# A hybrid GLA/SSD/mLSTM trunk on one core: product of decays and scores in two parts, and five small steps of the state-space loop moved between ScalarE, VectorE, SyncE and TensorE

## What is computed

```python
y, ss_f, ss_b = bidir_scan(ch, bh * dt[0], bh * dt[1], xh, log_a[0], log_a[1], init[2], init[3])
y = y + xh * d_skip[None, :, None, None]
y = y.transpose(0, 2, 1, 3).reshape(b, l, SSD_INNER) * jax.nn.silu(z)
y = rmsnorm(y.reshape(b, l, SSD_GROUPS, SSD_INNER // SSD_GROUPS), ...)
```

## Time and profile before

| | |
|---|---|
| median of three runs | 2345.26 us |
| profiled execution | 2342.83 us, of which the recorded span is 2341.1 us |
| TensorE busy in the span | 2271.2 us (97%) |
| VectorE, ScalarE, GpSimd busy | 1369.8, 905.7, 1054.2 us |
| mean granted clock of TensorE, of full speed | 0.988 |
| the loop over the heads 2 to 15 on ScalarE | 596.9 to 703.5 us from the span's start |
| start of the second half of the output projection on TensorE | 718.8 us |

### The profile page before, as it was taken

One profiled execution on the slowest core, in us unless ns is written; L12 is line 12 of the kernel. 1 busy time (PEld: TensorE's weight loads), 2 busy tenths in 40 slices (PEclk: granted clock), 3 DMA queues, 4 the chain that ended last, 5 costly groups with the idle time before them and its releaser, 6 DMA issues.

```text
span 2341.1 us, 32702 instructions
## 1 busy us (share of the span) xinstructions
PE 2271.2 (97%) x11907; PEld 1961.2 (84%) x11907; DVE 1369.8 (59%) x1750; ACT 905.7 (39%) x1979; POOL 1054.2 (45%) x815
## 2 busy tenths in 40 slices
PE   7999999999888999999999999999999999999998
PEld 6999999998437999999999999976555567888887
DVE  5995878854765457766757466653568753211113
ACT  5215435444892356746746252132330212101002
POOL 3353334324542345534534524455133135776664
PEclk9999999999899999999999999999999999999999
DMA  8953334254631134434534323354232222333332
GB/s 278 314 161 115 112 119 141 79 178 143 202 104 36 55 105 133 140 113 121 145 109 134 71 83 128 117 186 132 67 112 90 68 62 82 99 94 95 99 97 83
DMA packets 392724, 281.07 MB, mean 120 GB/s; under 512 B 33442, under 2 KB 357820, under 8 KB 392604
## 3 DMA queue, kind: packets, MB, share of 16 engines
q1 hardware_dynamic: 333420, 200.46, 28.8%
q10 hardware_dynamic: 59184, 78.99, 10.0%
HBM read 237.34 MB, written 42.07 MB: 119 GB/s over the span
## 4 chain that ended last, share of the span: by engine, by line
PE 80%; DVE 11%; ACT 5%; DMA 2%; issue 1%; POOL 1%; SPq 0%; ACTq 0%; DVEq 0%; POOLq 0%
PE PS L963 54%; PE PS L1046 4%; PE PS L1486 3%; PE PS L1684 3%; PE PS L1498 2%; PE PS L1632 2%; PE PS L1141 1%; DVE Gn L2591 1%; DVE stage L2547 1%; PE PS L1107 1%; ACT Dm L2086 1%; DVE xcr L2547 1%; ACT Db L2079 1%; PE PS L1125 1%; PE PS L1597 1%
## 5 line engine op out<-in xcount | busy, mean ns | idle before, releaser
L963 PE MATMUL PS<-act_hi,w_hi 128*128 128x384 f32 (+1 forms) x1824 | 637.6, 350 | 6.3 <-ACT act_hi L2147 2.8
L963 PE MATMUL PS<-act_hi,w_lo 128*128 128x384 f32 (+1 forms) x1824 | 630.1, 345 | 0.0
L963 PE MATMUL PS<-act_lo,w_hi 128*128 128x384 f32 (+1 forms) x1824 | 625.9, 345 | 0.0
L745 POOL TENSOR_TENSOR w_hi<-w_raw,ones 128x128 fp32r<-128x128 f32 x232 | 127.8, 551 | 1044.9 <-DMA w_raw<-in_ffn_w 406.2
L748 POOL TENSOR_TENSOR w_lo<-w_raw,w_hi 128x1024 fp32r<-128x1024 f32 (+1 forms) x232 | 559.2, 2410 | 19.4
L963 PEld LDWEIGHTS PS<-act_hi,w_hi 128*128 128x128 f32 x1824 | 343.1, 188 | 28.7 <-issue 11.6
L963 PEld LDWEIGHTS PS<-act_lo,w_hi 128*128 128x128 f32 x1824 | 342.6, 188 | 15.1 <-issue 1.2
L963 PEld LDWEIGHTS PS<-act_hi,w_lo 128*128 128x128 f32 x1824 | 343.0, 188 | 13.8
L2162 ACT ACTIVATE fprod<-mf_ring,cs 128x128 f32<-128x128 f32 x896 | 267.9, 389 | 26.6 <-DVE mf_acc L2462 26.6
L2462 DVE TENSOR_REDUCE mf_acc<-fprod 128x128 f32<-128x1024 f32 x112 | 224.9, 2020 | 86.0 <-ACT fprod L2162 86.0
L746 POOL TENSOR_SCALAR w_hi<-w_raw 128x896 fp32r<-128x896 f32 (+1 forms) x232 | 233.0, 1004 | 0.0
(11 more groups left out here) (376 smaller groups left out, 3694.1 us busy)
## 6 DMA issues: line engine op xcount, KB each, us to landing
w_raw<-in_ffn_w SPq DMA_DIRECT2D x120, 512.0 KB, 4.0
mf_ring<-in_w_mod SPq DMA_DIRECT2D x56, 512.0 KB, 3.7
w_raw<-in_a_w_in SPq DMA_DIRECT2D x44, 512.0 KB, 4.3
proj<-stage ACTq DMA_DIRECT2D x44, 384.0 KB, 4.3
w_raw<-in_b_w_up SPq DMA_DIRECT2D x32, 512.0 KB, 4.6
m_ring<-in_w_mod SPq DMA_DIRECT2D x12, 1024.0 KB, 9.1
rows<-g_d SPq DMA_DIRECT2D x16, 768.0 KB
m_raw<-in_w_mod SPq DMA_DIRECT2D x4, 2048.0 KB, 11.9
```

What stands on the lines that cost most here:

```text
L745: pool.tensor_tensor(w_hi[:, s, 0], w_raw[:, s, 0], ones[:], ALU.mult)
L963: last = pe.matmul(to[:, c0:c1], w[:, s, k, :], x[:, k, c0:c1], start=k == 0 and w is w_hi and x is hi, stop=k == kt - 1 and w is w_lo)
```

## The change

It has six parts. The product of `Dm` with `cb` becomes two instructions, of columns 0 to 1023 (counted in `m_first`) and 1024 to 2559 (`m_done`), and `pair_products` waits for them, and for `cross_done`, one after another ahead of the products that need them. `x_copies` of the pairs 2 to 7 goes to VectorE, behind `output` of the pair before. The squares of pairs 0 to 3 go to VectorE, ahead of the heads 10 to 13. The loads of `xt` for the pairs 3 to 7 go to SyncE, behind the rows of heads 6, 8, 10, 12 and 14. On ScalarE, `act_hi` of tile 0 is written before the square of pair 7. Two waits that the moved steps no longer need where they were go with them.

```diff
--- before.py
+++ after.py
@@ -411,6 +411,7 @@
         xt_in = [sem(f"ssd_xt_in{i}") for i in range(3)]
         g_out, G_OUT0 = x_in, 32
         z_late, Z_LATE0 = r_nbd, 2
+        m_first, M_FIRST0 = r_low, 2
         z_back, Z_BACK0 = tab_in, 16 * len(table_loads(a))
         b1_in, B1_IN0 = mod_in[0], 32
         rows_in, ROWS_IN0 = mod_in[1:3], 16
@@ -672,6 +673,9 @@
                         sp.wait_ge(mask_done, 2 * h - 2)
                         sp.wait_ge(back_mask, h - 1)
                         load_rows(h)
+                        if h >= 6 and h % 2 == 0:
+                            sp.wait_ge(y_mm, h // 2 - 2)
+                            sp.dma_start(xt[h // 2 % 3][:], proj0[X0 + h // 2]).then_inc(xt_in[h // 2 % 3], 16)
                         if h == 3:
                             sp.wait_ge(mm_done, n0)
                             for p in range(2):
@@ -1297,9 +1301,12 @@
                     pe.wait_ge(y_done, p - 1)
                 for c0, c1 in ((0, LAT), (LAT, T)):
                     pe.matmul(y[:, c0:c1], skip[:, p % 2], xt[p % 3][:, c0:c1], start=True, stop=False)
-                pe.wait_ge(m_done, 2 * p + 2)
-                pe.wait_ge(cross_done, 2 * p + 2)
+                pe.wait_ge(m_first, M_FIRST0 + 2 * p + 2)
                 for c in range(6):
+                    if c == 2:
+                        pe.wait_ge(m_done, 2 * p + 2)
+                    if c == 4:
+                        pe.wait_ge(cross_done, 2 * p + 2)
                     for f in range(2):
                         h = 2 * p + f
                         D = Dm[h % 4][:, c * LAT:c * LAT + LAT] if c < 4 else Dx[h % 4][:, (c - 4) * LAT:(c - 3) * LAT]
@@ -2050,8 +2057,6 @@
                 act.activation(out, bank((6, 7, 0, 1, 4, 5, 6)[i] if g else (4, 5, 4, 5, 4, 5, 7)[i]), ACT.Copy).then_inc(cb_put, 1)
 
             def x_copies(p):
-                if p >= 2:
-                    act.wait_ge(y_mm, p - 1)
                 act.activation(skip[:, p % 2], ident[:], ACT.Copy, scale=dcol[:, p:p + 1]).then_inc(skip_put, 1)
                 act.wait_ge(xt_tr, p + 1)
                 act.activation(xtok[:, p % 2].rearrange("p c f -> p (c f)"), slot(3), ACT.Copy).then_inc(xt_put, 1)
@@ -2088,8 +2093,6 @@
 
             def square(p):
                 act.wait_ge(y_done, p + 1)
-                if p == 3:
-                    act.wait_ge(sq_add, SQ_ADD0 + 1)
                 act.activation(sq_of[p][:], yT[:, p], ACT.Square).then_inc(ysq_done, 1)
 
             for i in range(7):
@@ -2113,32 +2116,19 @@
             x_copies(1)
             backward_decays(4)
             for p in range(2, PAIRS):
-                if p == 6:
-                    act.wait_ge(cb_put, 14)
-                    act.wait_ge(cb_mm, 14)
-                    for i in range(3):
-                        square(i)
                 decays_of(2 * p, range(6))
                 diagonal_decays(2 * p)
-                if p == 6:
-                    square(3)
-                if p == 2:
-                    x_copies(2)
                 if p == 4:
                     for i in SECOND:
                         group_copy(1, i)
                 backward_decays(2 * p + 1)
                 decays_of(2 * p + 1, range(6))
-                if p + 1 < PAIRS:
-                    act.wait_ge(y_mm, p - 1)
-                    act.dma_start(xt[(p + 1) % 3][:], proj0[X0 + p + 1]).then_inc(xt_in[(p + 1) % 3], 16)
                 diagonal_decays(2 * p + 1)
                 if p + 1 < PAIRS:
                     backward_decays(2 * p + 2)
-                    x_copies(p + 1)
             root(T, 4 * P, 3, 0)
             act.wait_ge(y_mm, PAIRS - 1)
-            for p in range(4, PAIRS):
+            for p in range(4, PAIRS - 1):
                 square(p)
             act.wait_ge(y_mm, PAIRS)
 
@@ -2146,7 +2136,9 @@
                 act.wait_ge(yn_done, t + 1)
                 act.activation(act_hi[:, t], yT[:, t], ACT.Copy).then_inc(nhi_done, 1)
 
-            for t in range(4):
+            normed_high(0)
+            square(PAIRS - 1)
+            for t in range(1, 4):
                 normed_high(t)
             root(T, 4 * P, 3, 1)
             for t in range(4, 8):
@@ -2796,7 +2788,8 @@
                 chain(dve.tensor_tensor(f, f, x, ALU.add), fb_done)
                 dve.wait_ge(dve_own, chain.n[dve_own])
                 dve.wait_ge(cb_put, 14 if h >= 8 else 7)
-                dve.tensor_tensor(D[:], D[:], cb[:], ALU.mult).then_inc(m_done, 1)
+                dve.tensor_tensor(D[:, 0:2 * LAT], D[:, 0:2 * LAT], cb[:, 0:2 * LAT], ALU.mult).then_inc(m_first, 1)
+                dve.tensor_tensor(D[:, 2 * LAT:DM], D[:, 2 * LAT:DM], cb[:, 2 * LAT:DM], ALU.mult).then_inc(m_done, 1)
                 if h in (1, 8):
                     context_weights(h)
                 if h == 1:
@@ -2807,6 +2800,20 @@
                 if h >= 4:
                     dve.wait_ge(y_mm, h // 2 - 1)
                 dve.tensor_tensor(Dx[h % 4][:], bank(4, 2 * LAT), cbx[:], ALU.mult).then_inc(cross_done, 1)
+
+            def x_copies(p):
+
+                dve.wait_ge(y_mm, p - 1)
+                dve.tensor_tensor(skip[:, p % 2], ident[:], dcol[:, p:p + 1].broadcast_to([P, P]), ALU.mult).then_inc(skip_put, 1)
+                dve.wait_ge(xt_tr, p + 1)
+                dve.tensor_copy(xtok[:, p % 2].rearrange("p c f -> p (c f)"), slot(3)).then_inc(xt_put, 1)
+
+            def first_square(p):
+
+                dve.wait_ge(cb_mm, 14)
+                if p == 3:
+                    dve.wait_ge(sq_add, SQ_ADD0 + 1)
+                dve.tensor_tensor(sq_of[p][:], yT[:, p], yT[:, p], ALU.mult).then_inc(ysq_done, 1)
 
             def output(p):
 
@@ -2820,12 +2827,16 @@
             dve.wait_ge(ct_put, 1)
             residual("out0", 0, 2, T, tiles=(4,))
             for p in range(PAIRS):
-                head_weights(2 * p)
-                head_weights(2 * p + 1)
+                for h in (2 * p, 2 * p + 1):
+                    if 10 <= h < 14:
+                        first_square(h - 10)
+                    head_weights(h)
                 if p + 1 == PAIRS:
                     rstd_diagonal(T)
                 if p:
                     output(p - 1)
+                    if p + 1 < PAIRS:
+                        x_copies(p + 1)
             def normed(t):
                 g = t // 4
                 if t % 4 == 0:
```

## The result

The changed kernel takes 2350.56 us (median of 20 runs, 2346.31 to 2358.64), the kernel before in the same rounds 2343.64 us (20 runs). The ratio is 1.0029, 95% interval 1.0020 to 1.0038: slower by about 6.8 us. The profiled execution took 2346.31 us, the fastest of the 20, with a span of 2344.5 us; that is 3.4 more than the span before, and not 6.8.

What follows compares the result with a forecast made beforehand. ScalarE was taken to pace the loop, with TensorE busy behind it; the change makes VectorE the slower. Lateness 3.9 + 2.95 + 4.5 - 1.5 - 1.8 = +8.05 us, so 2345.3 + 8.0 = 2353.3, range 2343 to 2359.

Steps and rivals of the forecast that it cites:

- Up to output 2: Loop start to pair 2's output: VectorE later by 1.1 (weight split at head 4) and 0.6 (mask in head 7's product).
- Second group: Second group of scores: first piece waits for VectorE's token-major copy 4, until 647.8; lateness +3.9 us, swallowing what came before.
- Head 9 to 10: VectorE without a gap: split product 0.87, copies 1.14, square 0 0.90, with the waits' own delays +2.95 us.
- Head 10 to 14: VectorE takes 34.4 us instead of 29.9, with split products, copies, three squares and waits for GpSimd: +4.5.
- 30.1 and four times 1: Heads 10 to 14: two pairs of 13.7 plus three squares of 0.9, and four GpSimd waits of about 1 us each.
- Head 14 to 15: VectorE takes 5.0 us here instead of ScalarE's 6.49: -1.5.
- Loop's end: End of loop: early products of pair 7 gain nothing; `act_hi` ahead of its square starts the projection 1.8 us earlier.
- the faster one: Rival in the loop: ScalarE stays last and VectorE absorbs the work in idle time; -5.7 us, 2339.6; chance 0.15.
- that VectorE keeps its port: About-the-same rival: no GpSimd mask between product parts, heads 9 to 13 lose 0.8 less each; +4.0, 2349.3; chance 0.20.
- The slower one: Rival: TensorE waits longer within pairs, its clock falls in pairs 3 and 4; +12 to +13, 2357.8; chance 0.10.
- the opposite chance: Behind the loop: early parts shorten TensorE's waits, the clock does not fall, and 1.6 us may come back.
- TensorE's early start counts only where TensorE is last: In the loop's pairs: the split product lets TensorE start 1.7 us earlier, a gain only where TensorE is last.

Runs made afterwards that it cites:

- copies alone: Only the copies and skip diagonals of pairs 2 to 7 moved to VectorE, against the kernel before; ratio 1.0004.
- the mask behind the product: Changed kernel, but GpSimd's backward mask waits for the whole product of two heads before, not its sums; ratio 1.0014 against the kernel before.
- the parts alone: Kernel before with only the product in two instructions and TensorE's graded waits; ratio 1.0015.
- the decays later in the changed kernel: Changed kernel, but TensorE's context decays come after the second quarter of products in pairs 0 to 6; ratio 1.0038 against the kernel before.

## Why the prediction was right

The forecast was 2353.3 with a range from 2343 to 2359, slower with 0.65; measured were 2350.56, and +6.8 (0.0029) against a forecast of +8.0. In the loop's traces it was +6.6. That 6.6 stands so near 6.8 is in part luck: the clock behind the loop gave 1.5 back, which the sum did not hold, so the trace accounts for 5.1, and 1.7 of the 6.8 are open, within the scatter of these traces. The forecast also came out near by errors that met. By the steps of the sum, each as lateness against before with the 0.94 taken off:

- **Up to output 2**: forecast +1.7, measured -0.9 (643.64 less 0.94, against 643.63). This step failed. The first sum of head 4 did meet the weight split, but took 1.96 and the second 0.41, where it was 2.59 for the second before, so head 4 was 0.3 later and not 1.1. And no mask got between the parts in the heads 4 to 8 (all 1.75): the rows of the heads 6, 7 and 8 landed when the second part had already started (0.4 to 0.9 us before), and the forward masks of head 8 waited until 642.70 for TensorE's pair 2. VectorE waits for ScalarE in head 7, and ScalarE had given away two copies of 0.98 by then; 0.9 of that shows.
- **Second group**: forecast first piece at 647.8, measured 645.6; product of head 8 forecast +3.9, measured 654.32 (655.26 less 0.94) against 651.09, +3.2. The mechanism was right. Two errors met: the copy was 2 us earlier, and the pieces were slower, since TensorE waited 3.20 ahead of them and the first four took 3.08 instead of 1.96.
- **Head 9 to 10**, from first sum to first sum: forecast +2.95, measured 8.59 (665.39 to 673.98) against 5.92, +2.67.
- **Head 10 to 14**: forecast 34.4, measured 673.98 to 707.03, 33.05 against 29.93: +3.1 in place of +4.5. The forecast's own terms, 30.1 and four times 1, add up to 34.1 and not to 34.4, which is 0.3 of the error; the waits for GpSimd, besides those of the masks between parts, were 3 and not 4 us. The one behind the sum of squares in head 13 is in them.
- **Head 14 to 15**: -1.5 forecast and measured (712.02 less 707.03 is 4.99).
- **Loop's end**, from head 15's first sum to the projection: forecast -1.8, measured -0.9 (14.36 against 15.24). The new order gave its 1.8, but TensorE came to the sums of squares late (pair 6 ended at 714.6), VectorE waited 0.51 for their root, and TensorE's early products of pair 7 stood in front of the spread until 719.3; that took 0.9 back.

The sum of the measured steps is 3.2 + 2.7 + 3.1 - 1.5 - 0.9 = 6.6. Of the rivals, the faster one fell with the measured time, and with copies alone; that VectorE keeps its port fell with the rows at 667.59 and with the mask behind the product. The slower one, TensorE's clock, was half right. The clock in the loop was lower (0.85 against 0.89), and below 1.00 in five of the eight pairs, but it was so in five pairs before as well; no cost of it shows where VectorE was last. Behind the loop the clock stayed up, which I had given as the opposite chance, for the wrong reason: I had put it to the early parts, and with the parts alone it was 0.63 there; it goes with the new order. The Trainium skill, "TensorE: Matmul & The Clock Gate", What's actually happening, says that the throttled state is the default and that activity releases it. The trace agrees: 0.85 in the loop, where TensorE stands up to 4.9 us at a time, and 1.00 behind it, where it stands 1.03. What I missed is the stand ahead of the context decays, 20.0 us in all in the changed kernel. I wrote that TensorE's early start counts only where TensorE is last; with the parts alone it seems to cost (by the traces; the ratios overlap), as it splits a pair's products by a wait. That did not change the sum, since VectorE covered it: with the decays later in the changed kernel nothing was gained.

## What to carry to other kernels

When work moves off the engine that is always busy, add it up on the receiver for each turn of the loop, with the port's waits, and look for what waits behind the place where it is put: one copy, behind the work of two heads, cost about as much as all six together. An instruction in two parts lets another engine in between, and starts a consumer early only if the consumer has nothing else to wait for in the middle. The cheapest gain here, 0.0021, came with the order of two steps ahead of the engine that everything waits for (run together with the loads).

## What the runs showed of the hardware

- A waiting instruction of GpSimd's runs between two VectorE instructions that follow at once: second parts of 2.41 us with a mask waiting, 3.38 with a sum of squares and 1.75 with nothing. The Trainium skill, "SBUF — State Buffer", Who interferes with whom, calls the port that the two engines share an exclusive lock, held for the whole instruction; the trace agrees, and cutting an instruction cuts the lock.
- The skip diagonal, 128 columns, took 0.29 us alone on VectorE, 0.91 beside a mask and 0.93 beside a sum of squares: here a small instruction lost most in proportion.
- TensorE's clock behind the loop went with the idle time ahead of it: 1.03 or 1.04 us and no fall in nine traces, 2.81 us and a fall in four of five. A fall cost 1.5 us.
